# Twelve slab pairs: high weights against high and low operand parts in one 512-column matmul, halves added behind it

## The reference

```python
def _odd_mixer(h, w_in, c_w, c_b, c_scale, w_out):
    p = h @ w_in                          # 2048 -> 4096
    v, z = jnp.split(p, 2, axis=-1)
    pooled = _causal_pool_means(v) - v    # trailing windows 2, 4, 8, 16 for four channel groups
    g = pooled.reshape(bsz, s, N_POOL_GROUPS, G_C)
    g = jnp.einsum("bsgc,gcd->bsgd", g, c_w) + c_b
    y = g.reshape(bsz, s, W_C) * c_scale
    return (y * jax.nn.silu(z)) @ w_out
```

## Time and profile before

| | |
|---|---|
| median of 3 executions | 1319.17 us (1318.1 to 1319.45) |
| the profiled execution | 1319.22 us, its span 1317.4 us |
| PE busy | 1305.6 us, 99% of the span |
| DVE busy | 987.8 us, 75% |
| ACT busy | 507.5 us, 39% |
| POOL busy | 138.2 us, 10% |
| granted PE clock | 0.998 |

### The profile page before, as it was taken

The page is one execution under the profiler, slowest core; times in us unless marked ns, Lnnn a source line. Parts: engine busy times, 40 slices in busy tenths (PEclk is TensorE's granted clock), DMA queues, the critical chain, the costliest instruction groups (busy, mean ns, idle before and its releaser), DMA issues. The chain is left out here.

```text
span 1317.4 us, 16646 instructions
## 1 busy us (share of the span) xinstructions
PE 1305.6 (99%) x6910; PEld 1130.0 (86%) x6910; DVE 987.8 (75%) x946; ACT 507.5 (39%) x557; POOL 138.2 (10%) x125
## 2 busy tenths in 40 slices
PE   9999999999999999999999999999999999999997
PEld 7888888888888888888888899899999999888886
DVE  6489998769755644544975887858878888799888
ACT  6521232221222121233565654234444445555552
POOL 0000000000007600000000100001213232000001
PEclk9999999999999999999999999999999999999999
DMA  9724443333357889761775564424434444764157
GB/s 323 224 65 112 112 114 108 90 101 96 96 162 240 256 260 293 229 225 41 268 294 195 188 180 128 133 73 118 130 110 126 139 132 158 258 223 160 46 211 255
DMA packets 234034, 219.75 MB, mean 167 GB/s; under 512 B 4016, under 2 KB 192560, under 8 KB 228976
## 3 DMA queue, kind: packets, MB, share of 16 engines
q1 hardware_dynamic: 227936, 208.42, 50.8%
q10 hardware_dynamic: 4512, 5.42, 1.2%
q0 software_dynamic: 1520, 4.98, 1.0%
HBM read 192.85 MB, written 25.95 MB: 166 GB/s over the span
## 5 line engine op out<-in xcount | busy, mean ns | idle before, releaser
L905 PE MATMUL bank<-h_hi,w_hi 128*128 128x512 f32 (+1 forms) x1536 | 545.6, 355 | 1.4 <-DVE w_lo L1671 1.0
L907 PE MATMUL bank<-h_lo,w_hi 128*128 128x512 f32 (+1 forms) x1536 | 543.8, 354 | 0.0
L909 PE MATMUL bank<-h_hi,w_lo 128*128 128x512 f32 (+1 forms) x1536 | 543.7, 354 | 0.0
L905 PEld LDWEIGHTS bank<-h_hi,w_hi 128*128 128x128 f32 x1536 | 290.8, 189 | 42.9 <-issue 1.8
L907 PEld LDWEIGHTS bank<-h_lo,w_hi 128*128 128x128 f32 x1536 | 290.8, 189 | 40.3 <-issue 0.7
L909 PEld LDWEIGHTS bank<-h_hi,w_lo 128*128 128x128 f32 x1536 | 290.8, 189 | 40.1
L1671 DVE TENSOR_TENSOR w_lo<-raw,w_hi 128x2048 fp32r<-128x2048 f32 x64 | 154.2, 2410 | 51.7 <-ACT w_hi L1200 51.6
L1200 ACT ACTIVATE w_hi<-raw 128x2048 fp32r<-128x2048 f32 x64 | 122.2, 1910 | 150.6 <-PE bank L909 131.3
L905 PE MATMUL bank<-w_hi,h_hi 128*128 128x512 f32 x448 | 174.6, 390 | 0.2 <-DVE rows L1950 0.2
L907 PE MATMUL bank<-w_lo,h_hi 128*128 128x512 f32 x448 | 174.3, 389 | 0.0
L909 PE MATMUL bank<-w_hi,h_lo 128*128 128x512 f32 x448 | 174.3, 389 | 0.0
(11 more groups left out here) (162 smaller groups left out, 1442.9 us busy)
## 6 DMA issues: line engine op xcount, KB each, us to landing
raw<-e_in SPq DMA_DIRECT2D x52, 1024.0 KB, 5.8
raw<-o_in SPq DMA_DIRECT2D x20, 1024.0 KB, 6.2
scratch<-e_out SPq DMA_DIRECT2D x17, 1024.0 KB, 7.2
spare<-e_out SPq DMA_DIRECT2D x12, 1024.0 KB, 7.5
rows<-o_in SPq DMA_DIRECT2D x12, 1024.0 KB, 6.0
spare<-o_out SPq DMA_DIRECT2D x12, 1024.0 KB, 7.3
scratch<-o_out SPq DMA_DIRECT2D x10, 1024.0 KB, 5.1
e_sums<-scratch SPq DMA_DIRECT2D x8, 1024.0 KB, 4.9
```

The source lines that it names most:

```text
L905: nc.tensor.matmul(dst, w[0], m[0], start=first, stop=False, skip_group_check=goes_on)
L907: nc.tensor.matmul(dst, w[0], m[1], start=False, stop=False, skip_group_check=goes_on)
L909: return nc.tensor.matmul(dst, w[1], m[0], start=False, stop=last, skip_group_check=goes_on)
```

## The change

In `half_product` the high weights now meet the high and low operand parts in one matmul: the moving operand is `[P, 2, 256]`, the result 512 columns of the bank. The low weights still meet the high part in 256 columns, accumulated on the first half. So a half product is 8 times (one matmul of 512 and one of 256 columns), and a bank holds two halves that have to be added behind it. For this, h_hi and h_lo, w_hi and w_lo, t1_hi and t1_lo become halves of one buffer each, and p1, p5, p1_p6 become 512 columns wide; the latter lies over `ident` and `ones`, which are done with by then. The three `keep` copies take 512 columns; v11, v12 and z22_sum each become an add of 512 columns and, after its result, an add of 256 columns. z21 can no longer go from the bank through SiLU: ACT copies one half (`copy_z21`), DVE adds the other from the bank (`z21_sum`, behind `prepared(f + 4)` at X22), ACT takes the SiLU (`silu_z21`). The SiLU of z22 moves ahead of the p5 copy. The diff, without the declarations of semaphores and the buffers that only change place:

```diff
-            return bank[4 * (p % 2) + n][:, 0:HALF]
+            return bank[4 * (p % 2) + n][:, :]
...
                 for k in range(KH):
-                    last = product(dst, (hi[:, k * P:(k + 1) * P], lo[:, k * P:(k + 1) * P]),
-                                   (m[0][:, k * HALF:(k + 1) * HALF],
-                                    m[1][:, k * HALF:(k + 1) * HALF]),
-                                   fresh and k == 0, k == KH - 1, True)
+                    both = m[:, :, k * HALF:(k + 1) * HALF]
+                    nc.tensor.matmul(dst, hi[:, k * P:(k + 1) * P], both,
+                                     start=fresh and k == 0, stop=False, skip_group_check=True)
+                    last = nc.tensor.matmul(dst[:, 0:HALF], lo[:, k * P:(k + 1) * P],
+                                            both[:, 0, :], start=False, stop=k == KH - 1,
+                                            skip_group_check=True)
...
-                pair_bank_free(p, 0, z21_silu)
+                pair_bank_free(p, 0, z21_ready)
...
-                    nc.scalar.activation(p1, y, ACT.Copy).then_inc(p1_kept, 1)
+                    nc.scalar.activation(p1[:, :], y, ACT.Copy).then_inc(p1_kept, 1)
                 elif kind == S1:
                     act.wait_ge(form_done, f + 1)
-                    act.wait_ge(z22_ready, p)
-                    nc.scalar.activation(p5, u, ACT.Copy).then_inc(p5_kept, 1)
+                    if p > 0:
+                        silu_z22(p - 1)
+                        act.wait_ge(z22_silu, p)
+                    nc.scalar.activation(p5[:, :], u, ACT.Copy).then_inc(p5_kept, 1)
                 elif kind == S2:
                     act.wait_ge(form_done, f + 1)
                     act.wait_ge(v12_ready, p)
-                    nc.scalar.activation(p1_p6, y, ACT.Copy).then_inc(p1_p6_kept, 1)
+                    act.wait_ge(z21_silu, p)
+                    nc.scalar.activation(p1_p6[:, :], y, ACT.Copy).then_inc(p1_p6_kept, 1)
...
+            def copy_z21(p):
+
+                act.wait_ge(form_done, AT_FORM[X22, p] + 1)
+                act.wait_ge(v12_ready, p + 1)
+                nc.scalar.activation(z21, pair_bank(p, 0)[:, HALF:T], ACT.Copy)\
+                    .then_inc(z21_copied, 1)
+
+            def silu_z21(p):
+
+                act.wait_ge(z21_ready, p + 1)
+                nc.scalar.activation(silu_row(PLAIN + p)[:, 0:HALF], z21, ACT.Silu)\
+                    .then_inc(z21_silu, 1)
...
                 if kind == X22:
-                    silu_halves(p)
+                    copy_z21(p)
                 else:
                     keep(f)
                 if f + RING <= last_form:
                     form_high(f + RING)
                 if kind == X22:
+                    silu_z21(p)
                     silu_scaled(p)
...
-                nc.vector.tensor_tensor(v_row[:, PAD:PAD + HALF], p1, pair_bank(p, 2), ALU.add)\
-                    .then_inc(v11_ready, 1)
+                link(nc.vector.tensor_tensor(p1[:, :], p1[:, :], pair_bank(p, 2), ALU.add))
+                nc.vector.tensor_tensor(v_row[:, PAD:PAD + HALF], p1[:, 0:HALF], p1[:, HALF:T],
+                                        ALU.add).then_inc(v11_ready, 1)
...
-                nc.vector.tensor_tensor(v_row[:, PAD + HALF:], p1_p6, pair_bank(p, 1), ALU.add)\
-                    .then_inc(v12_ready, 1)
+                link(nc.vector.tensor_tensor(p1_p6[:, :], p1_p6[:, :], pair_bank(p, 1), ALU.add))
+                nc.vector.tensor_tensor(v_row[:, PAD + HALF:], p1_p6[:, 0:HALF],
+                                        p1_p6[:, HALF:T], ALU.add).then_inc(v12_ready, 1)
...
-                nc.vector.tensor_tensor(z22, p5, pair_bank(p, 0), ALU.add).then_inc(z22_ready, 1)
+                link(nc.vector.tensor_tensor(p5[:, :], p5[:, :], pair_bank(p, 0), ALU.add))
+                nc.vector.tensor_tensor(z22, z22, p5[:, HALF:T], ALU.add).then_inc(z22_ready, 1)
+
+            def z21_sum(p):
+
+                dve.wait_ge(z21_copied, p + 1)
+                nc.vector.tensor_tensor(z21, z21, pair_bank(p, 0)[:, 0:HALF], ALU.add)\
+                    .then_inc(z21_ready, 1)
...
                 elif kind == S4:
                     v12(p)
+                elif kind == X22:
+                    z21_sum(p)
```

More of the change, by code:

```diff
@@ L156, in build @@
         h_at = free_from[0]
-        h_hi = sb("h_hi", [P, KT, T], F32R)
-        h_lo = sb("h_lo", [P, KT, T], F32R)
+        h_both = sb("h_both", [P, 2, KT, T], F32R)
+        h_hi, h_lo = h_both[:, 0], h_both[:, 1]
         rows = sb("rows", [P, KT, T])
@@ L161, in build @@
         raw = sb("raw", [P, RAW, SLAB])
-        w_hi = sb("w_hi", [P, SLOTS, SLAB], F32R)
-        w_lo = sb("w_lo", [P, SLOTS, SLAB], F32R)
+        w_both = sb("w_both", [P, 2, SLOTS, SLAB], F32R)
+        w_hi, w_lo = w_both[:, 0], w_both[:, 1]
         scratch_at = free_from[0]
@@ L170, in build @@
         vecs = sb("vecs", [P, NVEC])
-        ident = sb("ident", [P, P])
-        ones = sb("ones", [P, P])
         inv_count = sb("inv_count", [P, WINDOWS[-1]])
@@ L188, in build @@
         spare4 = sb("spare4", [P, SLAB], at=shifted_at)
[L189 to L192, removed]
+        ident_at = free_from[0]
+        ident = sb("ident", [P, P])
+        ones = sb("ones", [P, P])
+        sb("behind_ones", [P, T - 2 * P])
+        t1_both = sb("t1_both", [P, 2, SLAB], F32R, at=scratch_at + 8 * T * 4)
+        t1_hi, t1_lo = t1_both[:, 0], t1_both[:, 1]
+        p1 = sb("p1", [P, T], at=diagonals_at)
+        p5 = sb("p5", [P, T], at=junk_at)
+        p1_p6 = sb("p1_p6", [P, T], at=ident_at)
         sig, a_c, csum, mean, vsum, sq, _, x_rstd2, ln_rstd, sz0, sz1, x_rstd = (
@@ L217, in build @@
                       for form in (form_hi, form_lo))
+        form_both = h_both[:, :, :, :].rearrange("p b k t -> p b (k t)")
+        y_both = {name: form_both[:, :, n * SLAB:(n + 1) * SLAB]
+                  for n, name in enumerate(("y11", "y21", "y12", "y22"))}
+        t_both = {"t1": t1_both[:, :, :], "t2": w_both[:, :, 0, :], "t4": w_both[:, :, 3, :],
+                  "t3": y_both["y12"]}
         t_hi = {"t1": t1_hi[:, :], "t2": w_hi[:, 0, :], "t4": w_hi[:, 3, :], "t3": y_hi["y12"]}
@@ L222, in build @@
         v_row, sum_a, sum_b = (shifted[:, n, :] for n in range(3))
-        p1, p5 = kept[:, 0, :], kept[:, 1, :]
-        p1_p6, z22 = sums[:, 0, :], sums[:, 1, :]
+        z21, z22 = p1_p6[:, 0:HALF], p5[:, 0:HALF]
         v_buffer = (raw[:, 0, :], rows[:, 0:4, :].rearrange("p a c -> p (a c)"))
@@ L310, in build @@
         z22_ready = sem("z22_ready")
+        z21_copied = sem("z21_copied")
+        z21_ready = sem("z21_ready")
         z21_silu = sem("z21_silu")
@@ L1167, in _ @@
                 if g < 2:
-                    pe.wait_ge(z21_silu, PAIRS - 1 + g)
+                    pe.wait_ge(z21_ready, PAIRS - 1 + g)
                     pe.wait_ge(v12_ready, PAIRS - 1 + g)
@@ L1543, in keep, with silu_z22 @@
                     act.wait_ge(v12_ready, p)
-                    nc.scalar.activation(p1_p6, y, ACT.Copy).then_inc(p1_p6_kept, 1)
-            def silu_halves(p):
+                    act.wait_ge(z21_silu, p)
+                    nc.scalar.activation(p1_p6[:, :], y, ACT.Copy).then_inc(p1_p6_kept, 1)
+            def silu_z22(p):
                 j = PLAIN + p
-                act.wait_ge(form_done, AT_FORM[X22, p] + 1)
                 if j in SILU_OUT and j - 2 in SILU_OUT:
                     act.wait_ge(silu_stored[j % 2], 16 * ((j - SILU_OUT[0]) // 2))
-                nc.scalar.activation(silu_row(j)[:, 0:HALF], pair_bank(p, 0), ACT.Silu)\
-                    .then_inc(z21_silu, 1)
                 act.wait_ge(z22_ready, p + 1)
@@ L1633, in _ @@
             pooled_rounded(2)
-            silu_halves(PAIRS - 1)
+            silu_z22(PAIRS - 1)
+            copy_z21(PAIRS - 1)
             map_split(2, last_form)
+            silu_z21(PAIRS - 1)
             silu_scaled(PAIRS - 1)
@@ L2237, in z22_sum @@
                 dve.wait_ge(p5_kept, p + 1)
-                dve.wait_ge(z22_silu, p)
-                nc.vector.tensor_tensor(z22, p5, pair_bank(p, 0), ALU.add).then_inc(z22_ready, 1)
+                link(nc.vector.tensor_tensor(p5[:, :], p5[:, :], pair_bank(p, 0), ALU.add))
[4 more added lines that the diff above has]
+                    .then_inc(z21_ready, 1)
             def map_low(g):
@@ L2339, in can_finish @@
                 dve.wait_ge(resid_loaded[t], 32)
+            z21_sum(PAIRS - 1)
             pooled_low(8, 12)
```

4 lines of the change are left out of this document (2 added, 2 removed).

## The result

The changed kernel takes 1363.07 us (median of 4, 1361.0 to 1363.64) against 1318.72 us for the kernel before on the same chip: ratio 1.0331, 95% interval 1.0319 to 1.0344. It is 44.4 us slower; the forecast was 42.2 us more than before, 1361.4. The profiled execution has a span of 1361.8 us.

What follows compares the result with a forecast made beforehand. PE, busy 1305.6 of 1317.4 us, bounded the kernel; after the change DVE and ACT's loop would. Maps starting 41.3 us later, less 0.1, plus 1.0, gave 42.2 on 1319.17: 1361.4 us, range 1347 to 1371.

Steps and rivals of the forecast that it cites:

- The path leaves PE: In the pairs, DVE and ACT's loop takes 21.6 us without POOL against 19.4 us of PE, so PE waits.
- The loop's length: DVE and ACT's loop per pair: 22.9, 23.8 and 24.7 us with 2, 3 and 4 adds on POOL.
- The gap ahead of low X11: DVE idles 2.75 us per pair after z21_sum until ACT has rounded X11, where before it idled 1.04.
- The rival of 1339 us: In the pairs, the z21 exchange stays outside the loop, 22 us less over ten loops; chance 0.08.
- The added adds: On DVE, v11, v12 and z22_sum each take 0.72 us more and z21_sum adds 0.33: 2.5 us more per pair.
- POOL: POOL's running sums hold up DVE's two-input operations in the pairs: 1.3, 2.2 and 3.1 us with 2, 3 and 4 adds.
- PE's saving: In the pairs, a k tile goes from 0.360 to 0.3467 us on PE, 9.0 us in all, buying only longer waits.
- the rival of 1310 us: DVE's waits in the pairs take up the added work, PE stays the bound and gains 9.0 us; chance 0.05.
- The part behind the pairs: From the maps on, X22(11) gives 0.1 us back and DVE being further behind PE costs 1.0 (0 to 2.2).
- The rival of a falling clock: PE's clock falls to 1.2 GHz in the pairs, making a pair 38 us and the time over 1500 us; chance 0.02.
- The range: Whole kernel about 1347 to 1371 us, from bounds on POOL, the SBUF add and ACT's own waits, leaving rivals out.

Runs made afterwards that it cites:

- e1b: Changed kernel with three 256-column matmuls per k tile again, the start mark at a bank's first k tile only on the first half; 1361.8 us.
- e3: Changed kernel with z21 in a buffer of its own and its SiLU and scale behind the rounding of X11 in ACT's queue; 1334.3 us.
- e5: Changed kernel with POOL's running sums narrowed to 32 columns from the second pair on; 1341.8 us.
- e4: Kernel before with the change's half_product, joint buffers and 512-column banks, but its own copies and adds, second bank halves never read; 1314.7 us.
- e8: e4 with each half product's eight 512-column matmuls first, then its eight of 256 columns; 1314.9 us.
- e6: e3 with v12 and z21_sum moved into gaps of DVE's queue and z21's SiLU behind the rounding of S1; 1324.4 us.
- e10: e6 with the last pair's order changed in ACT's and DVE's queues, so pooled rows are rounded and their first low part taken earlier; 1324.6 us.
- e7: e4 with the 512-column matmul's moving operand read as one strip of the high part instead of two strips; 1314.1 us.
- e1: Changed kernel with three 256-column matmuls per k tile again, start marks on both halves of a bank at its first k tile; 1363.2 us.

## Why the prediction was right, step by step

- **The path leaves PE.** Right. DVE's idle time was taken for round trips with ACT and not for room, and the two queues were walked end to end. e1b shows that PE's work does not count. PE's list has 36.8 us of waits, under the 40 to 50 forecast: PE's own work was longer than assumed, by its pace (below) and by the stretches at half clock.
- **The loop's length.** 22.9, 23.8 and 24.7 us forecast; 22.97, 23.80 and 24.69 measured. Low X11(11) starts at 1119.29, forecast 1119.1. The last pair, from there to the maps, takes 32.6 us, forecast 32.0. The gap ahead of low X11: 2.75 forecast, 2.67 measured. The rival of 1339 us, in which the exchange over z21 stays outside the loop, is out: e3 had to move it, and gained 29 us.
- **The added adds.** The half add from SBUF, without a row before, takes 0.42 us beside nothing and 0.82 beside POOL; 0.41 plus a wait of 0.4 had been taken.
- **POOL.** The forecast of 0.9 us for each running sum, where the rows themselves gave 1.9 us per pair, is what put the forecast at 1361 rather than 1357. e5 took the width away, and by it POOL costs 1.3, 2.05 and 2.9 us per loop where 1.3, 2.2 and 3.1 were taken, while the rest of the loop is 21.7 to 21.8 us where 21.6 was. The two small errors have opposite signs, so part of the agreement to 0.1 us is luck. By the Trainium skill (SBUF — State Buffer, Who interferes with whom) the adds with one input in a bank should be free of it: L2267, at 0.68 us next to POOL's start, agrees. It is a weak test, since L2267 starts first (1032.64, POOL's sums at 1032.86).
- **PE's saving.** The term that was mis-sized: 0.0133 us per k tile, 9.0 us, forecast; 0.0067 us, 4.5 us, measured in e4. The rows it came from had equal neighbours, and where the two widths alternate a k tile takes 0.3533 us instead of 0.3467; e8 puts two thirds of that down to the alternation, the rest is open. It made no difference to the time, because none of the saving arrives; it would have made the rival of 1310 us read about 1315.
- **The part behind the pairs.** Forecast 0.9 us, measured 2.3 (209.9 against 207.6). What was missing is the clock: 4.98 us of waiting, then 1.2 GHz until 1155.4. Eight starts of 0.43 instead of 0.227 us are 1.6 us; with 0.7 us left for DVE being later, where 1.0 had been taken. The rival of a falling clock had been given 2 in 100 as a matter of the whole stage. In the form of a few microseconds it did happen, in the pairs too, where it costs nothing because DVE is later: the two loops of 24.69 us, one with such a stretch and one without, show it.
- **The range.** Its terms, as they are listed, give 1354 (4 and 3.5 us less) to 1368 (4.5 and 2 us more). 1347 to 1371 is 7 and 3 us wider, without a term for it. 1363.1 lies in either, so nothing hung on it.
- **The rival by which the waits take the added work up** (1310) fell with the first timeline. The added work did not find its way into DVE's gaps by itself; it had to be put there. e6 did this, PE was the pace of the pairs again, and the time came to 1324.

## What to carry to other kernels

When one engine is busy for 99% of the time and a change takes work off it by giving some to the others, the busy shares of the others don't say whether it fits. Look at what ends their gaps: where two queues hand work back and forth, walk one period of both queues with the new instructions in place and compare its length with the bound's; here a walk from rows was right to 0.1 us in 24, and each of its two parts, with and without POOL, to 0.2. An exchange between two engines that stands ahead of an instruction on which the other waits adds its round trip to the period: here 2.7 us a pair, and moving it behind that instruction was worth more (29 us) than taking away the added adds (25 us). When the loop is short enough again, look at the end of the stage: in e6 and e10 the loss had moved to the last pair and the maps behind it.

## What the runs showed of the hardware

- 512- and 256-column matmuls in turn, each with its own weights, take 0.3533 us together (e4); in runs of eight of a width 0.349 (e8); from stretches of one width 0.3467 would follow. Whether the 512 columns come from one strip or two makes no difference (e7, 234.6 us for the pairs as in e4).
- A start mark on the second half of a bank undoes the one on the first half (e1, results off by 0.32; right in e1b without that mark).
- A wait of PE of 4.98 us was followed by a stretch at a granted clock of 0.50, to 1155.4 us, in a kernel whose clock was 0.998 before. The Trainium skill (TensorE: Matmul & The Clock Gate, Part 1) has an idle PE as the cause, and this trace agrees as far as it goes: the five stretches at 0.50 in the pairs and the maps each come near a wait of PE, but of the eleven waits for z22 most have no such stretch. In e10 the 5 us from 1126, behind the wait of 4.1 us, have 0.66.
- A 256-column add with two SBUF inputs takes 0.82 us instead of 0.42 when it meets the start of a POOL add; with POOL's adds narrowed to 32 columns it takes 0.42 again (e5).
